# Scoring the cached keys of a sparse-attention decoder two chunks at a time on eight small matrix tiles

## The reference, cut to what matters

```python
logits = jnp.einsum('btgrd,btgksd->btgrks', q, ks) * SM_SCALE + bias      # selected blocks, per kv group g
p = _masked_softmax(logits, dist >= 0 and valid)
o_s = jnp.einsum('btgrks,btgksd->btgrd', p, vs)
logits = jnp.einsum('btgrd,blgd->btgrl', q, k) * SM_SCALE + bias          # window of 512
p = _masked_softmax(logits, (dist >= 0) & (dist < WINDOW))
o_w = jnp.einsum('btgrl,blgd->btgrd', p, v)
```

## Time and profile before

| what | us |
|---|---|
| runs of the kernel before | 921.92, 923.6, 924.26 |
| profiled execution, its own time | 921.69 |
| its span, first to last instruction | 919.7 |
| TensorE busy | 877.9 |
| VectorE busy | 603.5 |
| ScalarE busy | 367.5 |

### The profile page before, as it was taken

One profiled execution on the slowest core, in us unless ns is written; L12 is line 12 of the kernel. 1 busy time (PEld: TensorE's weight loads), 2 busy tenths in 40 slices (PEclk: granted clock), 3 DMA queues, 4 the chain that ended last, 5 costly groups with the idle time before them and its releaser, 6 DMA issues.

```text
span 919.7 us, 15492 instructions
## 1 busy us (share of the span) xinstructions
PE 877.9 (95%) x5973; PEld 554.8 (60%) x5973; DVE 603.5 (66%) x1131; ACT 367.5 (40%) x842; POOL 121.0 (13%) x129
## 2 busy tenths in 40 slices
PE   6999999999999999999899999998798999999997
PEld 4656665666666666767676776775555666544443
DVE  4688879999788988998566657666853444221222
ACT  4311252310021201025787787776745665310111
POOL 1011110000001011100103112232262221000000
PEclk9999999999999999999999999999999999999999
DMA  8444651422144166440930000000039898522211
GB/s 302 176 138 145 218 186 49 61 51 73 42 137 174 34 218 240 161 160 0 329 159 1 2 2 1 2 1 2 1 120 413 326 369 312 181 91 83 80 61 43
DMA packets 32108, 118.30 MB, mean 129 GB/s; under 512 B 3433, under 2 KB 11771, under 8 KB 22971
## 3 DMA queue, kind: packets, MB, share of 16 engines
q0 software_dynamic: 9360, 68.16, 20.0%
q1 hardware_dynamic: 19053, 43.39, 13.7%
q10 hardware_dynamic: 3623, 5.76, 2.9%
HBM read 108.33 MB, written 13.29 MB: 132 GB/s over the span
## 4 chain that ended last, share of the span: by engine, by line
PE 87%; DVE 4%; ACT 3%; issue 2%; DMA 2%; DVEq 1%; POOL 1%; ACTq 0%; POOLq 0%
PE PS L834 35%; PE PS L2078 12%; PE PS L1603 6%; PE PS L1613 6%; PE PS L1631 5%; PE PS L810 3%; PE PS L1929 3%; PE PS L1908 3%; ACT main L1411 2%; PE PS L1940 2%; PE PS L1963 2%; DMA main<-in_sel_v_dram,row 1%; PE PS L1586 1%; PE PS L799 1%; DVE main L1455 1%
## 5 line engine op out<-in xcount | busy, mean ns | idle before, releaser
L834 PE MATMUL PS<-main 128*128 128x352 f32 (+1 forms) x1056 | 330.1, 472 | 0.0
L834 PEld LDWEIGHTS PS<-main 128*128 128x128 f32 x1056 | 201.4, 191 | 120.7 <-issue 3.5
L1411 ACT ACTIVATE main<-PS,main 128x512 f32<-128x512 f32 (+3 forms) x192 | 104.0, 562 | 50.2 <-DVE main L1451 25.1
L2078 PE MATMUL PS<-main 128*128 128x512 f32 x256 | 112.3, 593 | 0.1
L435 ACT ACTIVATE main<-PS 128x384 f32<-128x384 f32 x24 | 11.8, 491 | 206.0 <-PE PS L834 199.7
L1613 PE MATMUL PS<-cst,main 128*128 128x128 f32 x528 | 73.6, 282 | 15.0 <-ACT main L1411 12.5
L645 DVE SCALAR_TENSOR_TENSOR main<-main,par 128x1022 f32<-128x1022 f32 (+16 forms) x66 | 83.8, 1270 | 5.3 <-issue 0.4
L2078 PEld LDWEIGHTS PS<-main 128*128 128x128 f32 x256 | 47.6, 190 | 56.4 <-issue 56.4
L604 DVE TENSOR_TENSOR main<-main 128x1024 f32<-128x1024 f32 x64 | 75.5, 1221 | 7.4 <-DMA main<-in_cmp_k_dram,row 4.2
L607 DVE TENSOR_TENSOR main<-main 128x1024 f32<-128x1024 f32 (+2 forms) x96 | 75.0, 781 | 7.2
L1613 PEld LDWEIGHTS PS<-cst,main 128*128 128x128 f32 x528 | 57.5, 142 | 30.4 <-ACT main L1411 23.0
(11 more groups left out here) (318 smaller groups left out, 1007.4 us busy)
## 6 DMA issues: line engine op xcount, KB each, us to landing
main<-in_w_tiles_dram SPq DMA_DIRECT2D x24, 512.0 KB, 3.6
out_dram<-main SPq DMA_DIRECT2D x18, 256.0 KB, 2.0
main<-in_x_prompt_dram SPq DMA_DIRECT2D x8, 512.0 KB, 9.3
main<-in_w_out_dram SPq DMA_DIRECT2D x4, 1024.0 KB, 6.4
main<-in_x_prompt_dram SPq DMA_DIRECT2D x16, 256.0 KB, 2.9
out_dram<-main SPq DMA_DIRECT2D x4, 512.0 KB
diag<-in_win_k_dram SPq DMA_DIRECT2D x8, 256.0 KB, 7.4
diag<-in_win_v_dram SPq DMA_DIRECT2D x8, 256.0 KB, 8.0
```

Of the source, the lines that this page charges most:

```text
L834: last = pe.matmul(bank(3 * s + j)[:, 0:w], ring[:, s, k * P:(k + 1) * P], xT[:, k, t0:t0 + w], start=(k == 0), stop=(k == KD - 1))
L1411: last = act.activation(prob[:, k % 2, g, h * nk_ * P:(h + 1) * nk_ * P], score_set(k, g)[:, h * nk_ * P:(h + 1) * nk_ * P], ACT.Exp, scal ...
L2078: last = pe.matmul(out_bank(m, h), proj[:, MIX[k], n * P:(n + 1) * P], wo[:, k, h * 512:(h + 1) * 512], start=(x == 0), stop=(x == KD - 1))
```

## The change

- A round is five slots instead of nine: chunks (0, 1), (2, 3), (4, 5), (6, 7) and the window. In a slot TensorE turns the exponentials of two chunks, then the keys of the next slot's two chunks, then scores its own two chunks, then does the values of two.
- A score product is 64 rows by 32 columns instead of 128 by 32: only the rows of its kv group. Even chunks have group g at rows 64g, odd chunks have the groups swapped, so that the eight products of two chunks stand on eight different tiles of the array. They write two PSUM banks, one for each chunk, 32 partitions for each product.
- The keys of an odd chunk have their halves swapped on the way out of PSUM. ScalarE, which took 128 by 1024 in one instruction, now takes each sample's bank by itself (two instructions of 128 by 512, or of 64 by 512 for an odd chunk), and VectorE copies the other 64 rows of an odd chunk, 64 by 1024. Once, in the prompt's stage, VectorE also copies the queries to the other half of the rows.
- `ktc` holds four chunks instead of two. TensorE turns each half of a chunk's keys when ScalarE has emptied that bank, and, for the first half, when VectorE has copied the chunk before.
- The semaphores of the two samples' loads are joined. ScalarE takes two pieces of the exponentials at the end of a round instead of one.

The diff, cut to its core:

```diff
-        ktc = proj_flat[:, QT * TOK:QT * TOK + 2 * 1024].rearrange("p (a b n) -> p a b n", a=2, b=2)
+        ktc = proj_flat[:, QT * TOK:QT * TOK + 4 * 1024].rearrange("p (a b n) -> p a b n", a=4, b=2)
...
+                if b == 4:
+                    dve_swapped_queries(dve)
...
+        SLOTS = [(0, 1), (2, 3), (4, 5), (6, 7), (NC,)]
+
+        def after(r, d):
+
+            return (r, SLOTS[d + 1]) if d + 1 < len(SLOTS) else (r + 1, SLOTS[0])
+
+        def swapped(c):
+            return c < NC and c % 2 == 1
+
+        def swapped_to(r, c):
+
+            return r * NC // 2 + min(c + 1, NC) // 2
+
+        def dve_swapped_queries(dve):
+
+            for g in range(G):
+                there, here = slice((1 - g) * HD, (2 - g) * HD), slice(g * HD, (g + 1) * HD)
+                dve.tensor_copy(qbd[there, :, 32 * g:32 * (g + 1)], qbd[here, :, 32 * g:32 * (g + 1)])
+            dve.drain().then_inc(SEM["q_swapped"], 1)
...
-                act.wait_ge(SEM["kt_ps"], k_no(r, c) + 1)
-                if k_no(r, c) >= 2:
-                    act.wait_ge(SEM["sd_ps"], k_no(r, c) - 1)
-                act.activation(ktc[:, k_no(r, c) % 2].rearrange("p b n -> p (b n)"), bank(KEYS, 2), ACT.Copy).then_inc(SEM["kt_sb"], 1)
+                k = k_no(r, c)
+                for b2 in range(2):
+                    act.wait_ge(SEM["kt_ps"], 2 * k + b2 + 1)
+                    if b2 == 0 and k >= 4:
+                        act.wait_ge(SEM["sd_ps"], k - 3)
+                    o, i = ktc[:, k % 4, b2, :], keys_bank(b2)
+                    if swapped(c):
+                        o, i = o[0:HD], i[HD:2 * HD]
+                    act.activation(o, i, ACT.Copy).then_inc(SEM["kt_act"], 1)
...
+                for d in range(len(SLOTS)):
+                    if p == 0 and d == 0:
                         act.wait_ge(SEM["oz"], NT)
-                    if p >= 0 and c % 2 == 0:
-                        turned(act, p, c)
-                    if c == NC and r < 4:
+                    if p >= 0:
+                        turned(act, p, 2 * d)
+                    r2, chunks = after(r, d)
+                    if r2 < 4:
+                        keys(r2, chunks[0])
+                    if p >= 0 and d < NC // 2:
+                        exp(p, 2 + d)
+                    if r < 4 and d == NC // 2:
                         exp(r, 0)
-                    if after(r, c)[0] < 4:
-                        keys(*after(r, c))
+                        exp(r, 1)
+                    if r2 < 4 and len(chunks) > 1:
+                        keys(r2, chunks[1])
...
+            def keys(r, c):
+                k = k_no(r, c)
+                dve.wait_ge(SEM["kt_ps"], 2 * k + 2)
+                if k >= 4:
+                    dve.wait_ge(SEM["sd_ps"], k - 3)
+                dve.tensor_copy(ktc[HD:2 * HD, k % 4].rearrange("p b n -> p (b n)"), bank(KEYS, 2)[0:HD]).then_inc(SEM["kt_dve"], 1)
...
+                for d, mine in enumerate(SLOTS):
                     if p == 0 and d == 0:
                         dve.wait_ge(SEM["oz"], NT)
...
                     if rnd == 0 and rest:
                         dve_side(dve, rest.pop(0))
+                    r2, chunks = after(r, d)
+                    if r2 < 4 and len(chunks) > 1:
+                        keys(r2, chunks[1])
                     if r < 4:
-                        peak(r, c)
+                        for c in mine:
+                            peak(r, c)
...
-            if k_no(r, c) >= 1:
-                pe.wait_ge(SEM["kt_sb"], k_no(r, c))
+            k = k_no(r, c)
             for b2 in range(2):
                 src = kd[:, b2, c * 512:(c + 1) * 512] if c < NC else kw_d[:, b2, :]
+                if k >= 1:
+                    pe.wait_ge(SEM["kt_act"], 2 * k - 1 + b2)
+                    if b2 == 0:
+                        pe.wait_ge(SEM["kt_dve"], swapped_to(r, c - 1)) if swapped_to(r, c - 1) else None
...
+            def scores(r, chunks):
+                k = k_no(r, chunks[-1])
+                if k >= 2:
+                    pe.wait_ge(SEM["sd_used"], k - 1)
+                pe.wait_ge(SEM["kt_act"], 2 * k + 2)
+                pe.wait_ge(SEM["kt_dve"], swapped_to(r, chunks[-1]))
...
                 for b2, g, q in QUARTERS:
-                    last = pe.matmul(scores_bank(r, c)[q:q + 32, :], qbd[:, 2 * r + b2, 32 * g:32 * (g + 1)], ktc[:, k_no(r, c) % 2, b2, :], start=True, stop=True)
-                last.then_inc(SEM["sd_ps"], 1)
+                    for c in chunks:
+                        at_ = (1 - g if swapped(c) else g) * HD
+                        last = pe.matmul(scores_bank(r, c)[q:q + 32, :], qbd[at_:at_ + HD, 2 * r + b2, 32 * g:32 * (g + 1)],
+                                         ktc[at_:at_ + HD, k_no(r, c) % 4, b2, :], start=True, stop=True)
+                        if (b2, g) == (1, G - 1):
+                            last.then_inc(SEM["sd_ps"], 1)
...
                     if p >= 0:
+                        turn(p, 2 * d)
+                        turn(p, 2 * d + 1)
+                    if d == 1 and p >= 1:
                         result(p - 1)
+                    if r2 < 4:
+                        pe_decode_keys_turn(pe, r2, chunks[0])
                     if rnd == 0 and rest:
                         pe_side(pe, rest.pop(0))
+                    if r2 < 4 and len(chunks) > 1:
+                        pe_decode_keys_turn(pe, r2, chunks[1])
```

More of the change, by code:

```diff
@@ new lines, in scores @@
+            def scores(r, chunks):
[4 more added lines that the diff above has]
+                pe.wait_ge(SEM["kt_dve"], swapped_to(r, chunks[-1]))
+                if r == 0 and chunks[0] == 0:
+                    pe.wait_ge(SEM["q_swapped"], 1)
+                for b2, g, q in QUARTERS:
+                    for c in chunks:
[4 more added lines that the diff above has]
+                            last.then_inc(SEM["sd_ps"], 1)
@@ L1956, in values @@
                 if c in (0, NC // 2, NC):
-                    for b2 in range(2):
-                        pe.wait_ge(vw_ld[b2], 16 * p + 16) if c == NC else pe.wait_ge(vd_ld[2 * (c // (NC // 2)) + b2], 16 * p + 16)
+                    pe.wait_ge(vw_ld if c == NC else vd_ld[c // (NC // 2)], 32 * p + 32)
                 if c <= NC:
@@ L1986, in pe_decode @@
             rest = list(TAIL_SIDES)
+            pe_decode_keys_turn(pe, 0, 1)
             for rnd in range(ROUNDS):
                 r, p = rnd, rnd - 1
-                for c in range(NC + 1):
+                for d, mine in enumerate(SLOTS):
+                    r2, chunks = after(r, d)
                     if p >= 0:
-                        turn(p, c)
-                    if c == NC and p >= 0:
-                        turn(p, NC + 1)
-                    if after(r, c)[0] < 4:
-                        pe_decode_keys_turn(pe, *after(r, c))
-                    if c == 2 and p >= 1:
+                        turn(p, 2 * d)
+                        turn(p, 2 * d + 1)
+                    if d == 1 and p >= 1:
                         result(p - 1)
-                    if rnd == ROUNDS - 1:
-                        next(output)
+                    if r2 < 4:
+                        pe_decode_keys_turn(pe, r2, chunks[0])
                     if rnd == 0 and rest:
                         pe_side(pe, rest.pop(0))
+                    if r2 < 4 and len(chunks) > 1:
+                        pe_decode_keys_turn(pe, r2, chunks[1])
+                    if rnd == ROUNDS - 1:
+                        for c in mine:
+                            next(output)
                     if r < 4:
-                        scores(r, c)
+                        if NC - 1 in mine:
+                            new_scores(r)
+                        scores(r, mine)
                     if p >= 0:
-                        if c == 0:
+                        if d == 0:
                             blocks(p)
-                        if c == NC:
+                        if NC in mine:
                             new_values(p, 0)
-                        values(p, c)
-                        if c == NC:
+                        for c in mine:
+                            values(p, c)
+                        if NC in mine:
                             new_values(p, 1)
@@ L2065, in pe_output_steps @@
         def pe_output_steps(pe):
-            pe.wait_ge(SEM["kt_sb"], 4 * (NC + 1))
+            pe.wait_ge(SEM["kt_act"], 8 * (NC + 1))
+            pe.wait_ge(SEM["kt_dve"], 2 * NC)
             for m, n in enumerate(OUT):
```

67 lines of the change are left out of this document (27 added, 40 removed).

## The result

The changed kernel takes 933.02 us (median of 4 runs, 931.92 to 933.39) where the kernel before takes 923.72: a ratio of 1.0101, interval 1.0083 to 1.0119. It is slower by 1%. The forecast was 923.4 us, range 918.5 to 930, so the time lies outside it. The profiled execution takes 932.95 us, its span 931.0 (before: 921.69 and 919.7), 11.3 us more.

A forecast was written before the change was run, and what follows sets the result against it. The prediction took the loads to bound the samples' rounds until about 702 us, and TensorE from then to 804. A loss of 6.3 us against gains of 6.4 or 6.5 gave 923.4 us, range 918.5 to 930.

The forecast's parts named there:

- Scores 0.93: TensorE's slots: eight score products of two chunks on eight tiles take 0.93 us, against 1.76 for two chunks before.
- Rival (a): Scores: row tiles sharing a bank do not overlap, two chunks take 1.76 us; 10.0 us more, 933.4 us; chance 0.12.
- Keys 2.30, with 0.48 behind ScalarE: TensorE's slots: keys of two chunks take 2.30 us, the second chunk waiting 0.48 for ScalarE to empty the banks.
- VectorE's copy 1.22: VectorE's added copy of 64 by 1024 keys in a slot takes 1.22 us, hidden behind TensorE in later rounds.
- rival (b): VectorE decides: its copy across partition halves takes up to twice 1.22 us; 928.6 us in all; chance 0.17.
- Sides late, first indirect load at 688.1, keys at 697.4: Round 0: VectorE's queue delays the sides, so GpSimd's first indirect DMA and pair 1's keys come 5.2 us later.
- A second wait of 1.8 us for the other half of the keys: Round 1: the keys' second half lands at 709.3 but is wanted at 707.5, costing 1.8 us more.
- The clock: TensorE behind its wait for pair 1's keys: work priced at the earlier trace's durations, with no term for clock.
- With no idle time between: TensorE's rounds before the change: one chunk's period of 2.90 us was read as holding no idle time.
- The sum: Whole kernel: loss 6.3 us, gains 6.4 or 6.5, net -0.2 us; 923.4 against the median of 923.6.
- Turn of chunk 2 in round 1: TensorE in round 1: this turn starts at 706.5 instead of 702.02, 4.5 us later.
- the loss of 6.3: Round 0 and the loads: 4.5 us until chunk 2's turn plus 1.8 for the keys' second half; bounds 2 and 9.

The follow-up runs named there:

- e8_slots: Kernel with sides early and 14 small products near 438 us, but without swapped groups and VectorE's copies of keys and queries: 929.17 us, 1.0024 to the kernel before.
- second run: The unaltered changed kernel, measured and profiled again on another chip: 932.36 us, ratio 1.0097 to the kernel before.
- e1_sides: Changed kernel with round 0's three side tasks all in its first slot on TensorE and VectorE: 924.88 us, ratio 1.0008 to the kernel before.
- e10_both_again: Changed kernel with sides early and 14 small products near 438 us, repeated on another chip: 918.05 us, ratio 0.9936 to the kernel before.
- e2_fill: Changed kernel with 14 filler products on TensorE ahead of its wait for pair 1's keys: 925.24 us, ratio 1.0023 to the kernel before.
- e4_light: Changed kernel without the second sample's selected loads in later pairs (stale data, a probe): 922.73 us, ratio 0.9992 to the kernel before.
- e11_changed_again: The unaltered changed kernel, measured again on another chip: 932.36 us, ratio 1.0097 to the kernel before.
- e3_pad: Changed kernel with 32 small products (128 instructions) added on TensorE near 438 us: 927.76 us, ratio 1.0042 to the kernel before.
- e5_both: Changed kernel with round 0's sides in its first slot and 14 small products near 438 us: 924.53 us, ratio 0.9970 to the kernel before.
- e6_pad56: Changed kernel with 14 small products (56 instructions) added on TensorE near 438 us: 929.55 us, ratio 1.0030 to the kernel before.
- e9_issue: Kernel with sides early and 14 small products, GpSimd's later key loads held until the slot's values are done: 919.51 us, 0.9952 to the kernel before.

## Why the prediction was wrong, step by step

- **Scores 0.93** (bounds 0.86 to 1.76): 1.02. Right. Rival (a) named 933.4 and the kernel takes 933.0, but its mechanism is absent; a time that fits proves nothing. Row tiles that write other partitions of one bank ran side by side here: 1.02 us for eight products on eight tiles, against 1.87 for the eight in e8_slots, whose two chunks share four tiles.
- **Keys 2.30, with 0.48 behind ScalarE**: the second chunk's keys start 1.29 after the first's (1.35 predicted). Right.
- **VectorE's copy 1.22**: right, and rival (b) is out. In the changed kernel, VectorE in round 1:

```profile
701.65 1.22 DVE L1908 COPY main<-PS 64x1024 f32<-64x1024 f32 x1 [7.80 <-PE PS L1949]
```

- **Sides late, first indirect load at 688.1, keys at 697.4**: it issued at 689.60 (687.87 in the second run, where the prompt's stage ended as early as before) and the keys were used from 697.84 (698.55 in the second run). So the issue came as the queue said, and from there to the use it took 8.2 and 10.7 us where 9.3 were predicted. The chain of the earlier trace rows has shifted, link by link:

```profile
685.94 0.68 DVE L1437 TENSOR_TENSOR main<-main,PS 128x512 f32<-128x512 f32 x1
686.70 1.27 POOL L1567 TENSOR_TENSOR main<-main 128x512 f32<-128x512 f32 x1 [2.37 <-DVE main L1437]
689.60 1.01 POOL L1733 DMA_INDIRECT main<-in_sel_k_dram,row  x1 [0.27 <-POOL main L1571]
```

- **A second wait of 1.8 us for the other half of the keys**: did not come here; TensorE got there late enough. With the sides early it did (0.7 us in e1_sides, 1.6 in e10_both_again).
- **The clock**: the sum has no term for it, and this failed first. The prediction itself put a wait of 7 us in front of TensorE and priced what stood behind it at the durations of a busy one:

```profile
697.84 3.77 PE L1949 MATMUL PS<-cst,main 128*128 128x128 f32 x16 [6.54 <-DMA main<-in_sel_k_dram,row]
701.54 1.93 PE L1978 MATMUL PS<-main,kcn 64*32 64x512 f32 x8
```

  From start to start 3.70 for the keys and 1.86 for the window's scores, where the busy TensorE of e2_fill took 2.36 and 0.99: 2.2 us. The third stall brought half clock again (785.4 to 792.2), 2.7 us by the same comparison with the rounds before.
- **"With no idle time between"**: this failed second, and weighs most. A timeline without idle time was taken for a property of the work; it also rested on the program's packets arriving in time. In the kernel before the latest of them (786.68) started 82 records ahead of the end of a block, counted as in the table above; in the changed one the three that stall started with 0, 4 and 0 records left. The slots use a round's records up sooner between the same loads, and move the loads against the blocks; which of the two counts for more is not shown.
- **The sum.** Turn of chunk 2 in round 1: 709.50, against 702.02 and 706.5 predicted. 7.5 later = 4.5 (predicted) + 0.4 (keys later than 697.4) + 2.2 (clock) + 0.4 (of it 0.3 for a value run of 1.39 us beside GpSimd's issue). From there to the end of the last round 105.4 us against 101.7, +3.8: stalls of 8.1 and 2.7 of clock, which leaves gains of 7.0 (6.5 predicted). Together 11.3. e4_light, without the stalls, confirms the gain of a round: 1.7 us. The gains came about, and of the loss of 6.3 the first 4.5; the 13.0 us of stalls and half clock that were not in the sum made it wrong.

## What to carry to other kernels

When a change makes an engine wait that did not wait, price what stands behind the wait too. Here TensorE's granted clock was 0.50 around the waits of 6.5 to 9.0 us in five runs, and 1.00 where the filler of e2_fill kept it busy. When a change packs TensorE's instructions closer between the same large loads, look for the program's own packets in the DMA records and count how late they come, before and after. Here the latest packet had 82 records to spare before the change; after it three had 0, 4 and 0, and the stalls behind them took 8.1 us. And when a result matches a rival's number, look for the rival's rows before believing it.

## What the runs showed of the hardware

- TensorE stood still where the program has no wait: 16 stalls of 1.4 to 4.2 us in eight profiled runs (the changed kernel and e11_changed_again three each, e1_sides three, e3_pad and e5_both two each, e6_pad56, e9_issue and e10_both_again one each), all at record numbers a multiple of 256 apart, each ending 2.2 to 2.5 us after a 16 KB packet of queue q8 that followed the one before by 7.7 to 11.4 us. That TensorE was out of program there is inferred from these numbers. 56 added instructions left one of three stalls (e6_pad56), and with the sides early one or two of three (e10_both_again, e5_both).
- The granted clock fell to 0.50 around every wait of 6.5 to 9 us for keys (6.54 in the changed kernel, 8.55 in e3_pad, 8.99 in e4_light, 7.66 in e6_pad56, 8.98 in e11_changed_again) and around the three stalls of 3.4 us and more (3.95 in the changed kernel, 3.40 in e1_sides, 4.22 in e11_changed_again). Of the 13 shorter stalls it fell behind three (1.91 us in e1_sides, 1.63 in e3_pad, 2.50 in e9_issue), and not behind one of 2.21 in the changed kernel: for short gaps these runs give no price that can be relied on.
- Beside indirect loads issued by GpSimd a dense run of TensorE's products took longer: 64 records in 1.21 to 1.39 us instead of 1.10, and on one chip 2.5 (e5_both, e6_pad56) and 1.65 (e8_slots).
- Times scatter differently: ten runs of the kernel with early sides lay between 920.75 and 929.83 us, ten of the one with lighter loads, which has one stall of 0.9 us, between 921.96 and 924.12. Stalls alone do not explain it: eight runs of the changed kernel, with three stalls each in the two that were profiled, lay between 931.82 and 933.39.
